# Recurrence in a four-layer transformer kernel: running sums and exponentials placed in PSUM banks

## What is computed

```python
def chunk_gated_recurrence(q, k, v, g):
    """S_t = diag(exp(g_t)) S_{t-1} + k_t outer v_t ; o_t = S_t^T q_t, in chunks of HG_CHUNK."""
...
        G = jnp.cumsum(gc, axis=2)
        o_inter = jnp.einsum('bhck,bhkv->bhcv', qc * jnp.exp(G), state)
        diff = G[:, :, :, None, :] - G[:, :, None, :, :]
        decay = jnp.exp(jnp.where(causal[:, :, None], diff, -jnp.inf))
        A = jnp.einsum('bhtsk,bhsk->bhts', qc[:, :, :, None, :] * decay, kc)
        o_intra = jnp.einsum('bhts,bhsv->bhtv', A, vc)
```

## Time and profile before

| | us |
|---|---|
| median of three runs | 3082.63 |
| the profiled execution, as timed | 3073.08 |
| its span, first to last instruction | 3071.2 |
| TensorE products busy | 2844.9 (93%) |
| VectorE busy | 1287.3 (42%) |
| ScalarE busy | 1232.4 (40%) |
| GpSimd busy | 2059.3 (67%) |

### The profile page before, as it was taken

How to read it: one execution, slowest core, us unless ns; L and a number is a source line. 1 busy time by engine, 2 the same in 40 slices (tenths; PEclk the granted TensorE clock), 3 DMA queues, 4 the chain that set the end, 5 groups by cost and what they waited for, 6 DMA issues and landing times.

```text
span 3071.2 us, 46378 instructions
## 1 busy us (share of the span) xinstructions
PE 2844.9 (93%) x18990; PEld 2598.2 (85%) x18990; DVE 1287.3 (42%) x1553; ACT 1232.4 (40%) x1538; POOL 2059.3 (67%) x896
## 2 busy tenths in 40 slices
PE   7999879999988987999999999889999999988998
PEld 6898678799877877879989899877998989988798
DVE  2651374623424137453243423756424232375523
ACT  4344424444424442444444433324444443333443
POOL 7777445788856644578888774337888877425786
PEclk9999989999999998999999999989999999999999
DMA  6455323555575542355555554125555555423554
GB/s 214 159 198 192 130 83 107 169 189 179 199 168 178 189 143 76 105 197 185 186 188 185 166 177 145 63 82 185 187 179 194 186 167 175 138 69 103 181 189 145
DMA packets 132106, 487.77 MB, mean 159 GB/s; under 512 B 14608, under 2 KB 14608, under 8 KB 130896
## 3 DMA queue, kind: packets, MB, share of 16 engines
q1 hardware_dynamic: 127296, 463.53, 45.1%
q0 software_dynamic: 4624, 21.48, 2.7%
HBM read 478.65 MB, written 6.29 MB: 158 GB/s over the span
## 4 chain that ended last, share of the span: by engine, by line
PE 77%; DVE 12%; DMA 3%; issue 3%; ACT 3%; POOL 1%; DVEq 0%; SPq 0%; POOLq 0%
PE psA L343 47%; PE psY L343 28%; DMA ring<-in_weights 3%; PE psT L394 2%; DVE Sc L1226 1%; DVE st L1221 1%; DVE arena L1300 1%; POOL rest L969 1%; ACT Sc L1697 1%; DVE xT_upper L1304 1%; DVE Sc L1216 1%; DVE x L1172 1%; DVE xT_rest L1305 1%; ACT upper L1697 1%; DVE Sc L1481 0%
## 5 line engine op out<-in xcount | busy, mean ns | idle before, releaser
L969 POOL TENSOR_TENSOR rest<-ring,upper 128x1024 fp32r<-128x1024 f32 (+1 forms) x832 | 2020.8, 2444 | 885.5 <-ACT upper L1697 876.8
L1697 ACT ACTIVATE upper<-ring 128x1024 fp32r<-128x1024 f32 (+1 forms) x832 | 867.9, 1051 | 967.5 <-DMA ring<-in_weights 966.5
L343 PE MATMUL psA<-xT_upper,upper 128*128 128x256 f32 x2944 | 412.7, 283 | 12.2 <-ACT upper L1697 9.2
L343 PE MATMUL psA<-xT_rest,upper 128*128 128x256 f32 x2944 | 413.9, 283 | 0.0
L343 PEld LDWEIGHTS psA<-xT_upper,upper 128*128 128x128 f32 x2944 | 385.7, 189 | 26.9 <-issue 9.9
L343 PE MATMUL psA<-xT_upper,rest 128*128 128x256 f32 x2944 | 406.4, 280 | 0.3 <-POOL rest L969 0.3
L1198 DVE TENSOR_TENSOR sil<-sil,psA 128x256 f32<-128x256 f32 x144 | 60.7, 421 | 802.6 <-ACT sil L1697 802.6
L343 PEld LDWEIGHTS psA<-xT_rest,upper 128*128 128x128 f32 x2944 | 380.5, 192 | 0.0
L343 PEld LDWEIGHTS psA<-xT_upper,rest 128*128 128x128 f32 x2944 | 373.6, 189 | 0.5 <-POOL rest L969 0.5
L343 PE MATMUL psY<-upper,hT_upper 128*128 128x512 f32 x704 | 206.9, 399 | 23.2 <-DVE hT_rest L1201 19.2
L343 PE MATMUL psY<-upper,hT_rest 128*128 128x512 f32 x704 | 208.0, 401 | 0.0
(11 more groups left out here) (234 smaller groups left out, 3530.1 us busy)
## 6 DMA issues: line engine op xcount, KB each, us to landing
ring<-in_weights SPq DMA_DIRECT2D x880, 512.0 KB, 3.4
G<-in_rows POOLq DMA_DIRECT2D x6, 1024.0 KB, 7.4
rel_by_distance<-G POOLq DMA_DIRECT2D x1, 4096.0 KB, 45.8
G<-in_rows POOLq DMA_DIRECT2D x7, 512.0 KB, 6.0
arena<-rel_by_distance POOLq DMA_DIRECT2D x1, 2048.0 KB, 14.2
x<-in_x SPq DMA_DIRECT2D x2, 512.0 KB, 5.6
par<-in_params POOLq DMA_DIRECT2D x4, 256.0 KB, 6.1
xn<-in_mem POOLq DMA_DIRECT2D x1, 1024.0 KB, 9.5
```

The lines of the kernel that those rows point to most:

```text
L343: i = pe.matmul(out, lhsT, rhs, start=start, stop=stop)
L969: pool.tensor_tensor(rest[:, r, 0:n], ring[:, r, 0:n], upper[:, r, 0:n], ALU.subtract)\
L1697: act.activation(out, in_, func, **kw).then_inc(*up)
```

## The change

The running sums, once made, are copied by ScalarE from `GC` into PSUM banks psY 0 and 1 (`GP`). The subtractions take `mid` from there and the other operand from `GC` as before; they still write `EB[i % 2]`. ScalarE writes the exponentials of all levels into psT 0 and 1 (`E`) and not in place; the products read them there, with `KH` and `QH` still in SBUF.

The waits follow: the scans raise a signal of their own; ScalarE's copy waits for it and for the last readers of the psY banks; `gaps(0)` waits for the copy; `gaps(i)` now waits for exponential i - 2, which reads the `EB` buffer, and no longer for `decayed(i - 2)`; exponential 0 waits for the last readers of psT; exponential i waits for `decayed(i - 1)`, since `E` has one buffer.

```diff
+        joined = lambda banks: banks.rearrange("p b c -> p (b c)").rearrange("p (h t) -> p h t", h=4)
+        E, GP = joined(psT[:, :, :]), joined(psY[:, 0:2, :])
...
-                    i.then_inc(*sig["vector step"].up())
-                dve.wait_ge(*sig["vector step"].value(sig["vector step"].count))
+                    i.then_inc(*sig["vector step"].up() if h < 3 else sig["sums made"].up(0))
+                dve.wait_ge(*sig["sums made"].after(0))
...
                     if i >= 2:
-                        dve.wait_ge(*sig["decayed"].after(i - 2))
-                        own()
-                    mid = g0[:, :, (1 << i) - 1:1 << i].broadcast_to(list(g0.shape))
+                        dve.wait_ge(*sig["decays"].after(i - 2))
+                    if i == 0:
+                        dve.wait_ge(*sig["sums copied"].after(0))
+                    mid = halves(GP, i)[0][:, :, (1 << i) - 1:1 << i].broadcast_to(list(g0.shape))
                     tt_(e0, mid, g0, ALU.subtract).then_inc(*sig["gaps"].up((i, 0)))
                     tt_(e1, g1, mid, ALU.subtract).then_inc(*sig["gaps"].up((i, 1)))
...
-                    e0, e1 = halves(EB[i % 2], i)
+                    e0, e1 = halves(E, i)
                     t0, t1 = halves(TL[i % 2], i)
                     tt_(t0, e0, halves(KH, i)[0], ALU.mult).then_inc(*sig["vector step"].up())
                     tt_(t1, e1, halves(QH, i)[1], ALU.mult).then_inc(*sig["decayed"].up(i))
...
+                for b in range(TT):
+                    act.wait_ge(*taken(("c", b)))
+                act.wait_ge(*sig["sums made"].after(0))
+                go(GP, GC, ACT.Copy, sig["sums copied"].up(0))
...
                 for i in range(8):
                     act.wait_ge(*sig["gaps"].after((i, 1)))
-                    go(EB[i % 2], EB[i % 2], ACT.Exp, sig["decays"].up(i))
+                    if i == 0:
+                        for h in range(2):
+                            act.wait_ge(*taken(("cT", 1, h)))
+                    else:
+                        act.wait_ge(*sig["decayed"].after(i - 1))
+                    go(E, EB[i % 2], ACT.Exp, sig["decays"].up(i))
                     gate_out(gates(("level", i)))
```

## The result

The changed kernel takes 3049.15 us, the median of 4 runs (3047.95 to 3056.34), beside 3081.66 us for the kernel before (3079.89 to 3084.58, 4 runs). The ratio is 0.9898 with a 95% interval of 0.9881 to 0.9916: 32.5 us less, where 3051 us was forecast. The profiled execution took 3049.43 us.

What follows compares the result with a forecast made beforehand. VectorE was taken to bound the kernel inside the recurrence's levels, not outside. Gains of 15.9 and 15.75 us, 31.7 in all, taken from the median 3082.63 gave 3051 us; range 3040 to 3056, 8 in 10 for 3040 to 3062.

Steps and rivals of the forecast that it cites:

- Part (1): In the levels, 64 VectorE subtractions and products read one operand from PSUM and take 0.68 us each, without stalls.
- the rule of the Trainium skill: Level 0 reads every other PSUM value, so would pay twice as much: 0.25 us a layer, making 3051.5 us.
- Parts (2) and (3): ScalarE writes exponentials to PSUM at 1.05 us; the added copy of the sums, 1.05 to 2.1 us a layer, costs 0.
- Part (4): One buffer of exponentials instead of two costs 0, covered by 1.1 us to spare in the level after a gate copy.
- Part (5): From level 0 TensorE goes at its own pace, 4.64 us a level, gaining 15.9 and 15.75 us in the two layers.
- The price of PSUM: Rival: PSUM costs twice where unseen, for exponential and products 3060 us, with subtractions too 3073 us; chance 0.13.
- the stall that stays: Rival: VectorE is still held up by its SBUF write or other SBUF operand, 3083 to 3086 us; chance 0.03.
- the turning point: Rival: VectorE's four level instructions cost over 1.38 us each, so slower than before, 3089 us at 1.5 us; chance 0.03.
- the weights: Rival: in the levels TensorE outruns weight splits or transfers, say 1 us a level, giving 3067 us; chance 0.03.

Runs made afterwards that it cites:

- the control's profile: The kernel before, run once more unchanged against the kernel before: ratio 0.9996, median 3074.82 us; its levels took 54.6 and 51.1 us in layers 0 and 1.
- the second comparison: The changed kernel run again as it stands, against the kernel before in a later session: ratio 0.9919, median 3047.37 us in 9 runs.

## Why the prediction was right

**Part (1), the operands.** Right in cause and size. Four experiments bound the cause from all sides: with one half in PSUM only that half runs free, with the same order in SBUF all four are stretched again, up to 2.88 us, and without GpSimd's work all four run free with all operands in SBUF. The price of 0.68 us held for what no row had shown: two banks in one instruction, and level 0's step of two in PSUM, where no instruction took over 0.70 us. By that, the 0.25 us a layer by the rule of the Trainium skill ("Advanced Engine Details and Errata", Memory Cachelines) didn't come.

**Parts (2) and (3), ScalarE into PSUM.** Taken at 1.05 us, measured 1.02 and 1.03. The copy lies at 359.38, right behind the scans, and hides as worked out.

**Part (4), the single buffer.** Right that it costs nothing; the cover was off. It is 0.89 us at the even levels behind a gate copy, not 1.1, because the sum let the gate copy start with the level's products and end 0.6 us later; it started at 387.19, 0.20 us after them, and all behind it moved by that. At level 0 there is no cover on ScalarE, because of the splits behind exponential 0. The change adds nothing there, so the forecast didn't suffer; a change that had added a microsecond to ScalarE would have been mispriced by it.

**Part (5), TensorE's pace.** 4.64 us from level to level in all fourteen steps, and 15.96 and 15.8 us won where 15.9 and 15.75 were worked out. The rest of the kernel did shift as a block within its scatter. What the sum didn't know is that one profile of before is one of two phases of the collisions: against the control's profile the same change wins 28 us in the levels.

**How good the number is.** That 3051 and 3049.15 us lie so near is partly luck. The two profiled spans differ by 23.6 us, 8 less than the sum; the second comparison gave 0.9919 (0.9890 to 0.9947), which is 16 to 34 us, and a median lower by 28.6. What the traces bear out to a tenth of a microsecond is the gain in the levels against the first profile, not the time of the whole kernel.

**The rivals.** The price of PSUM, the stall that stays and the turning point were each decided by the 64 durations; the weights by the lack of any wait for them beyond the first gate piece.

## What to carry to other kernels

Where VectorE's time for one and the same instruction jumps between its usual value and about one GpSimd instruction, look at its operands before its work: moving one of two SBUF operands to PSUM was enough, and ScalarE could make that copy at no cost. Count such a stall only where another engine waits for it, and work the gain out as the distance to the next engine's own pace, since two halves of a fix are worth less than twice one half. When adding waits, look for the place without cover, which here was the first level. A cast needs its one operand moved, and where it was not held up before, that makes it slower (0.69 us, not 0.43).

## What had not been expected

A stalled instruction waits for the end of the GpSimd instruction under way, however small it is itself. The chain of the changed kernel runs, in a feed-forward stage, through tiny steps on 128x4 elements, while GpSimd computes eight remainders. VectorE's time line and GpSimd's:

```profile
938.49 0.18 DVE L1381 RECIPROCAL arena<-arena 128x4 f32<-128x4 f32 x1
938.70 2.11 DVE L1382 TENSOR_TENSOR arena<-arena 128x4 f32<-128x4 f32 x1
940.85 2.32 DVE L1383 TENSOR_TENSOR arena<-arena 128x4 f32<-128x4 f32 x1
943.20 2.32 DVE L1384 TENSOR_TENSOR arena<-arena 128x4 f32<-128x4 f32 x1
...
947.85 2.27 DVE L1386 TENSOR_SCALAR arena<-arena,par 128x4 f32<-128x4 f32 x1
```

```profile
931.09 19.00 POOL L971 TENSOR_TENSOR rest<-ring,upper 128x1024 fp32r<-128x1024 f32 x8 [1.96 <-ACT upper L1700]
```

The two products and the sum of four elements take 2.1 to 2.3 us, near GpSimd's 2.38 for one remainder, since each begins just after the one before was let go; the reciprocal in front of them, with one operand, takes 0.18. One SBUF operand is not safe for every operation: the multiplication by a column of parameters (L1386) took 2.27 us, and the cast of the earlier trace rows 9.82, as long as four remainders.

And the stop works both ways. A product of a level recorded 0.07 us behind GpSimd's start was held for 2.90 us, one recorded 0.09 us behind it was not held, and GpSimd was. Over a layer that made 54.6 or 51.1 us out of one and the same program. What decides between them is finer than these records show.
